# Streaming encoder layer with grouped experts: expert weights with neighbouring rows in one partition, and edits to mixing and routing

## What is computed

```
aff = sigmoid(h @ w_router);  sel = aff + router_bias            # 16 experts in 4 groups
group = argmax over groups of the sum of its two best sel
idx   = the 2 best experts inside that group;  w = aff[idx] / sum
y     = sum over e of gates[:, e] * ((silu(h @ w_gate[e]) * (h @ w_up[e])) @ w_down[e])
x     = x + g2 * y
```

## Time and profile before

| | us |
|---|---|
| median of 3 runs | 1313.42 |
| lowest and highest run | 1308.0, 1316.89 |
| the profiled execution | 1310.96 |
| its span (first to last instruction) | 1309.2 |
| mixing, first level to last copy of logits | 431.6 to 735.8 |
| routing, first operation to first gather | 737.5 to 771.0 |
| experts | 771.0 to the end |

### The profile page before, as it was taken

The page is one execution under the profiler, slowest core; times in us unless marked ns, Lnnn a source line. Parts: engine busy times, 40 slices in busy tenths (PEclk is TensorE's granted clock), DMA queues, the critical chain, the costliest instruction groups (busy, mean ns, idle before and its releaser), DMA issues. The chain is left out here.

```text
span 1309.2 us, 21577 instructions
## 1 busy us (share of the span) xinstructions
PE 1154.3 (88%) x6971; PEld 945.9 (72%) x6972; DVE 733.6 (56%) x1079; ACT 555.5 (42%) x930; POOL 346.4 (26%) x427
## 2 busy tenths in 40 slices
PE   4799999999786999999999249999999999899974
PEld 1688979988564777777777237888887887678863
DVE  0763500352355678777776574546195586656861
ACT  1664411333333355555553034324074364534750
POOL 1001100122322444334431020333332341333222
PEclk9799999999757999999999659999999999989987
DMA  9727673512183533332221583775779889897874
GB/s 347 285 91 266 230 279 109 175 48 73 55 231 99 144 109 109 110 110 86 78 88 54 184 314 121 239 236 176 205 241 366 255 262 354 285 336 242 263 284 96
DMA packets 119943, 249.88 MB, mean 191 GB/s; under 512 B 18225, under 2 KB 47665, under 8 KB 116802
## 3 DMA queue, kind: packets, MB, share of 16 engines
q1 hardware_dynamic: 107778, 204.92, 45.1%
q0 software_dynamic: 12096, 44.05, 12.8%
HBM read 205.02 MB, written 43.93 MB: 190 GB/s over the span
## 5 line engine op out<-in xcount | busy, mean ns | idle before, releaser
L2183 PE MATMUL psum<-e_w_h,e_x_h 128*128 128x512 f32 x432 | 173.9, 402 | 19.6 <-DVE w_gu L2296 12.8
L2185 PE MATMUL psum<-e_w_h,e_x_l 128*128 128x512 f32 x432 | 170.9, 395 | 0.0
L2184 PE MATMUL psum<-w_gu,e_x_h 128*128 x432 | 170.6, 395 | 0.0
L2130 POOL DMA_INDIRECT out<-e_work,e_to x26 | 81.0, 3117 | 298.2 <-DVE e_work L2284 298.2
L2296 DVE TENSOR_TENSOR w_gu<-w_gu,e_w_h 128x1024 f32 x128 | 146.9, 1218 | 11.5 <-ACT e_w_h L2239 11.5
L2239 ACT ACTIVATE e_w_h<-w_gu 128x1024 fp32r x128 | 123.3, 1048 | 46.2 <-issue 35.9
L2183 PEld LDWEIGHTS psum<-e_w_h,e_x_h 128*128 128x128 f32 x432 | 82.8, 192 | 37.8 <-DVE w_gu L2296 13.3
L503 PE MATMUL psum<-p_w_h,p_h_h 128*128 128x512 f32 (+1 forms) x288 | 105.8, 367 | 3.8 <-DVE p_h_l L659 3.8
L505 PE MATMUL psum<-p_w_h,p_h_l 128*128 128x512 f32 (+1 forms) x288 | 105.0, 364 | 0.0
L504 PE MATMUL psum<-p_w_l,p_h_h 128*128 128x512 f32 (+1 forms) x288 | 104.9, 364 | 0.0
L2185 PEld LDWEIGHTS psum<-e_w_h,e_x_l 128*128 128x128 f32 x432 | 82.5, 191 | 17.8
(11 more groups left out here) (389 smaller groups left out, 2484.8 us busy)
## 6 DMA issues: line engine op xcount, KB each, us to landing
w_gu<-in_w_e_gate SPq DMA_DIRECT2D x32, 1024.0 KB, 11.9
w_gu<-in_w_e_up SPq DMA_DIRECT2D x32, 1024.0 KB, 14.0
w_dn<-in_w_e_down SPq DMA_DIRECT2D x16, 2048.0 KB, 15.0
shared<-in_w_ada SPq DMA_DIRECT2D x24, 1024.0 KB, 6.5
p_w_raw<-in_w_in SPq DMA_DIRECT2D x5, 2048.0 KB, 9.3
tok_d<-p_tok SPq DMA_DIRECT2D x27, 256.0 KB, 2.0
feat_d<-p_work SPq DMA_DIRECT2D x12, 576.0 KB, 3.4
p_work<-in_x SPq DMA_DIRECT2D x9, 512.0 KB, 3.7
```

The costliest lines, as they stand in the source:

```text
L2183: pe.matmul(psum[:, j, :], x_h[:, k, :], wh, start=(k == 0), stop=False)
L2184: pe.matmul(psum[:, j, :], x_h[:, k, :], wl, start=False, stop=False)
L2185: last = pe.matmul(psum[:, j, :], x_l[:, k, :], wh, start=False, stop=(k == KC - 1))
```

## The change

The expert loads put rows 8p to 8p+7 of gate and up (a half: 8p to 8p+3 or 8p+4 to 8p+7), and rows 4p to 4p+3 of down, into partition p. To match, `turn_x` turns the columns 8r+k of the gathered rows, and `turn_u` the columns 4r+k of u. In mixing the diagonal goes to bank OB (columns 256 to 263), level 0 no longer waits for `pair_clear`, the diagonal waits for `rec_kept`, and `turn4(OB, k_d)` stands ahead of level 6. In routing the bias is loaded in mixing, the tile counts are added by one scan over a matmul result ordered by expert, the list matmuls are F32R with the gate as a high and a low part (product and rest on GpSimd, copy on ScalarE), the row number carries the "not empty" mark (it is one higher), and `at_place` is made last.

```
@@ load_expert
-        ks, rows = slice(half * KC // 2, (half + 1) * KC // 2), slice(half * D // 2, (half + 1) * D // 2)
+        ks = slice(half * KC // 2, (half + 1) * KC // 2)
         for j, w in enumerate((d["w_gate"], d["w_up"])):
-            sp.dma_start(b["w_gu"][:, par, j, ks, :], w[one(e), rows, :].rearrange("a (k p) n -> p (a k) n", p=P)).then_inc(b["gu_loaded"][par][half], 16)
+            sp.dma_start(b["w_gu"][:, par, j, ks, :], w[one(e), :, :].rearrange("a (p k) n -> p (a k) n", p=P)[:, ks, :]).then_inc(b["gu_loaded"][par][half], 16)
...
-    sp.dma_start(b["w_dn"][:, par, :, :], d["w_down"][one(e), :, :].rearrange("a (k p) n -> p (a k) n", p=P)).then_inc(b["dn_loaded"][par], 16)
+    sp.dma_start(b["w_dn"][:, par, :, :], d["w_down"][one(e), :, :].rearrange("a (p k) n -> p (a k) n", p=P)).then_inc(b["dn_loaded"][par], 16)
@@ experts, turn_x and turn_u
-                    last = pe.transpose(psum[:, 2 + k // 4, (k % 4) * P:(k % 4 + 1) * P], x_g[:, par, k * P:(k + 1) * P], ident[:, :])
+                    last = pe.transpose(psum[:, 2 + k // 4, (k % 4) * P:(k % 4 + 1) * P], x_g[:, par, :].rearrange("p (r k) -> p k r", k=KC)[:, k, :], ident[:, :])
...
-                    last = pe.transpose(psum[:, 4, k * P:(k + 1) * P], u[:, k * P:(k + 1) * P], ident[:, :])
+                    last = pe.transpose(psum[:, 4, k * P:(k + 1) * P], u.rearrange("p (r k) -> p k r", k=KD)[:, k, :], ident[:, :])
@@ mixing
+            sp.dma_start(b["bias"][:, :], router_bias.partition_broadcast(P)).then_inc(b["bias_loaded"], 16)
...
-                if i == 0:
-                    pe.wait_ge(s["pair_clear"], t + 1)
-                else:
+                if i == 0 and t:
+                    pe.wait_ge(s["state_ready"], t + 1)
+                if n:
                     pe.wait_ge(s["pair_ready"], n)
...
+                    if t:
+                        pe.wait_ge(s["rec_kept"], t)
-                last = pe.matmul(psum[:, M0, 2 * c:2 * c + 2], prod[:, c * P:(c + 1) * P], head_cols[:, :], start=True, stop=True)
+                last = pe.matmul(psum[:, OB, DIAG + 2 * c:DIAG + 2 * c + 2], prod[:, c * P:(c + 1) * P], head_cols[:, :], start=True, stop=True)
...
-                level(t, 6)
                 pe.wait_ge(s["kexp_ready"], t + 1)
                 if t:
                     pe.wait_ge(s["logit_ready"], t)
                 turn4(OB, k_d, s["kd_turned"])
+                level(t, 6)
@@ route, GpSimd and ScalarE
+            pool.wait_ge(s["in_list_ready"], 1)
+            pool.tensor_tensor(gate[:, :, :], in_list[:, :, :], bc(w_k[:, :, :].rearrange("p k t -> p (k t)"), 2, SLOTS),
+                               ALU.mult).then_inc(s["gate_ready"], 1)
+            pool.wait_ge(s["gate_high"], 1)
+            pool.tensor_tensor(entry[:, :, 2, :], gate[:, :, :], entry[:, :, 1, :].bitcast(F32), ALU.subtract).then_inc(s["gate_low"], 1)
...
+            act.wait_ge(s["gate_ready"], 1)
+            nc.scalar.activation(entry[:, :, 1, :], gate[:, :, :], ACT.Copy).then_inc(s["gate_high"], 1)
@@ route, TensorE
-            pe.matmul(psum[:, 1, 0:NT * NE], ones[:, :], flat, start=True, stop=True).then_inc(s["counted"], 1)
+            pe.matmul(psum[:, 1, 0:NT * NE], ones[:, :], both[:, :, :].rearrange("p t e -> p e t"), start=True, stop=True).then_inc(s["counted"], 1)
+            pe.wait_ge(s["gate_low"], 1)
@@ route, VectorE
-            link(dve.tensor_copy(tile_sum[:, :, :].rearrange("p t e -> p (t e)"), psum[:, 1, 0:NT * NE]))
-            for t in range(1, NT):
-                link(dve.tensor_tensor(before[:, t, :], before[:, t - 1, :], tile_sum[:, t - 1, :], ALU.add))
-            link(dve.tensor_tensor(count[:, :], before[:, NT - 1, :], tile_sum[:, NT - 1, :], ALU.add))
+            link(dve.tensor_tensor_scan(through[:, :, :].rearrange("p e t -> p (e t)"),
+                                        keep[:, :, :].rearrange("p e t -> p (e t)"), psum[:, 1, 0:NT * NE], 0.0, ALU.mult, ALU.add))
...
-            dve.tensor_tensor(at_place[:, :, :], ...)
-            link(dve.tensor_tensor(in_list[:, :, :], ...))
-            dve.tensor_copy(entry[:, :, 2, :], in_list[:, :, :])
+            dve.tensor_tensor(in_list[:, :, :], ...).then_inc(s["in_list_ready"], 1)
+            dve.wait_ge(s["in_list_ready"], 1)
...
-            dve.tensor_tensor(entry[:, :, 1, :], in_list[:, :, :], bc(flat(w_k[:, :, :]), 2, SLOTS), ALU.mult).then_inc(s["entries_ready"], 1)
+            dve.tensor_tensor(at_place[:, :, :], ...).then_inc(s["entries_ready"], 1)
...
-            dve.tensor_copy(b["list_gate"][:, :], psum[:, 2, SLOTS:2 * SLOTS])
+            link(dve.tensor_copy(b["list_gate"][:, :], psum[:, 2, SLOTS:2 * SLOTS]))
+            link(dve.tensor_tensor(b["list_gate"][:, :], b["list_gate"][:, :], psum[:, 2, 2 * SLOTS:3 * SLOTS], ALU.add))
```

More of the change, by code:

```diff
@@ L59 @@
 LISTS = 2 * NT + NE - 1
[L60 removed]
+SLOTS = LISTS + 3
 ENDS, LAST, SPLIT, NTH, INFO_W = SLOTS, SLOTS + NE, SLOTS + NE + 1, 2 * SLOTS + NE + 1, 3 * SLOTS + NE + 1
@@ L173, in stream_layer @@
             sampling(nc, b, d, sinks, state_in, s_sample)
-            mixing(nc, b, d, x, sinks, s_prompt)
+            mixing(nc, b, d, x, sinks, s_prompt, router_bias)
         b.update(
@@ L1117, in _, with mixing @@
             dve.tensor_tensor(o_n[:, :], o_n[:, :], gate, ALU.mult).then_inc(s["ob_ready"], 1)
-def mixing(nc, b, d, x, sinks, s_prompt):
+def mixing(nc, b, d, x, sinks, s_prompt, router_bias):
     psum, ident, logit = b["psum"], b["ident"], b["logit"]
@@ L1126, in mixing @@
     GAPS = 3
+    DIAG = 256
     NU = NT
@@ L1804, in _, with route @@
             keep_logits(u)
-def route(nc, b, d, router_bias):
+def route(nc, b, d):
     psum, ident = b["psum"], b["ident"]
@@ L1818, in route @@
         NG4 = NT * NG
-        bias = sb("bias", [P, NE])
+        bias = b["bias"]
         aff, sel, tmp = (sb(n, [P, NT, NE]) for n in ("aff", "sel", "tmp"))
@@ L1828, in route @@
         ones = sb("ones", [P, P])
-        tile_sum, before = sb("tile_sum", [P, NT, NE]), sb("before", [P, NT, NE])
-        count, n_list, end, first, ones_e = (sb(n, [P, NE]) for n in ("count", "n_list", "end", "first", "ones_e"))
+        keep, through = sb("keep", [P, NE, NT]), sb("through", [P, NE, NT])
+        n_list, end, first, ones_e = (sb(n, [P, NE]) for n in ("n_list", "end", "first", "ones_e"))
         steps = sb("steps", [P, NT])
@@ L1838, in route @@
         row_no = sb("row_no", [P, NT])
-        at_place = sb("at_place", [P, 2 * NT, P])
+        at_place = sb("at_place", [P, 2 * NT, P], F32R)
         in_list = sb("in_list", [P, 2 * NT, SLOTS])
-        entry = sb("entry", [P, 2 * NT, 3, SLOTS])
+        entry = sb("entry", [P, 2 * NT, 3, SLOTS], F32R)
+        gate = sb("gate", [P, 2 * NT, SLOTS])
         place_no, empty = sb("place_no", [P, P]), sb("empty", [P, SLOTS])
@@ L1849, in route @@
         kind = sb("kind", [P, SLOTS], I32)
-        names = "bias_loaded pool_made chain nlogit_ready e_ready counted both_ready entries_ready lists_made".split()
+        names = "pool_made in_list_ready gate_ready gate_high gate_low chain nlogit_ready e_ready counted both_ready entries_ready lists_made".split()
         s = {n: sem(n) for n in names}
@@ L1952, in _ @@
             link(dve.tensor_tensor(first[:, :], end[:, :], n_list[:, :], ALU.subtract))
-            link(dve.tensor_tensor(place[:, :, :].rearrange("p t e -> p (t e)"), psum[:, 0, 0:NT * NE],
-                                   before[:, :, :].rearrange("p t e -> p (t e)"), ALU.add))
+            link(dve.tensor_tensor(place[:, :, :], psum[:, 0, 0:NT * NE].rearrange("p (t e) -> p t e", e=NE),
+                                   through[:, :, :].rearrange("p e t -> p t e"), ALU.add))
             link(dve.scalar_tensor_tensor(out=place[:, :, :], in0=bc(first[:, :], 1, NT), scalar=float(P), in1=place[:, :, :],
@@ L1965, in _ @@
             flat = lambda ap: ap.rearrange("p k t -> p (k t)")
-            dve.tensor_tensor(at_place[:, :, :], bc(place_no[:, :], 1, 2 * NT), bc(flat(place_f[:, :, :]), 2, P), ALU.is_equal)
-            link(dve.tensor_tensor(in_list[:, :, :], bc(list_no[:, :], 1, 2 * NT), bc(flat(list_f[:, :, :]), 2, SLOTS), ALU.is_equal))
-            dve.tensor_copy(entry[:, :, 2, :], in_list[:, :, :])
+            dve.tensor_tensor(in_list[:, :, :], bc(list_no[:, :], 1, 2 * NT), bc(flat(list_f[:, :, :]), 2, SLOTS),
+                              ALU.is_equal).then_inc(s["in_list_ready"], 1)
+            dve.wait_ge(s["in_list_ready"], 1)
             for k in range(2):
```

36 lines of the change are left out of this document (20 added, 16 removed).

## The result

The changed kernel takes 1304.14 us (median of 20 runs, 1298.15 to 1310.15) where the kernel before takes 1310.97 (20 runs beside it). The ratio is 0.9947, with a 95% interval of 0.9936 to 0.9959: half a per cent faster, 7 us, which is within 1%. The forecast was 1290, 21 us faster. The profiled execution has a span of 1303.9 us against 1309.2.

A forecast was written before the change was run, and what follows sets the result against it. TensorE, busy 88% of the span, was taken to bound the kernel, so its waits cost time directly. 1311.0 us less 16 (stalls), 5 (routing) and 0.5 (mixing) gave 1289.5, called 1290; range 1281 to 1320, forecast's own 1281 to 1300.

The forecast's parts named there:

- Stalls: Expert stage: TensorE's four waits behind late weight loads, 27 us in all; longer packets were to save 16 us.
- small stall: Expert stage, two places losing 2.7 and 3.1 us behind a late w_dn load; 2.5 us each to be saved.
- 2.5 us earlier: w_dn's load took 11.08 us, 5.9 over the bare transfer; longer packets were to win back 2.5 of these.
- I cost that at nothing: Expert stage: weights' longer turns make POOL's gathers slower, but about a step of cover hides it; 0 us.
- rival D: Expert stage: gathers starve behind 16 KB packets and turn_x waits for x; 1306 us or more, chance 0.05.
- Column step: turn_x and turn_u: transposes reading columns 32 and 16 bytes apart instead of 4 cost 0, at most 46 us.
- Rivals A and B: Transposes doubling in time: all stepped ones (A, 1324 us, chance 0.14) or only the 32 byte step (B, 1314, 0.20).
- Routing: Routing stage: shorter counts, entry path and list matmuls sum to 6.0 us; 5.0 taken, as the first gather meets loads.
- The entry path: Routing, from the start of in_list to TensorE, gate product on POOL: 5.0 us against 5.4, saving 0.4.
- Mixing: Mixing stage: level 0's saved wait returns at level 1, k_d's turn nets 0.1 us a tile; 0.5 saved in all.
- Rival C: Expert loads keep 2 KB and 4 KB descriptors, or larger ones don't win turns; 1305.5 us, chance 0.13.

The follow-up runs named there:

- vec_gate: Changed kernel without its mixing edits, with routing's gate product and low part made by VectorE instead of GpSimd; 0.9923 of the kernel before.

## Why the prediction was wrong, point by point

**Stalls, predicted 16 saved, measured 11.0: the largest step that failed.** The mechanism stood: packet for packet, shares of a third and two thirds where both queues have work, as the row of 1138 to 1141 shows before and after. Over the whole of the large stall's loads, 1120 to 1138, POOL's queue is often empty and the shift is smaller: SP's queue moved 3.99 MB before and 4.65 after, POOL's 1.88 and 1.67. (The Trainium skill, "DMA: Bandwidth & Descriptors", section on queues, rings and completion order, has 9 to 17 descriptors to a turn; the equal counts at three run lengths, 220 to 215, 109 to 109 and 163 to 165, say one.) What failed is the size of the saving and where I put it. "In each small stall that is nearly all that was lost", from w_dn "2.5 us earlier": in the first small stall w_dn was issued at 973.21 and taken by ScalarE at 984.58 before, at 974.49 and 985.86 after.

```profile
974.49 0.33 SPq L193 DMA_DIRECT2D w_dn<-in_w_e_down  x1
...
985.86 3.90 ACT L2262 ACTIVATE e_w_dh<-w_dn  x4 [7.75 <-DMA w_dn<-in_w_e_down]
```

That is 11.4 us both times. I had read the 5.9 us over the bare load as lost turns. In those 11.4 us SP's queue moved 2.95 MB before and 3.15 after, and POOL's only 1.0 either way: there was little for longer packets to win back. SP's bytes were already more than w_dn's 2.1, so parts of w_gu moved while some parts of w_dn were still out. The small stalls went from 5.8 us to 3.5, the large ones from 21.2 to 12.5 (expected: 0.8 and 10.2). In the large one the 2.5 us came nearly whole: w_dn, issued at 1120.69 and taken at 1132.62 before, was issued at 1121.21 and taken at 1130.88, 2.3 us sooner. And w_gu was taken at 1138.32 after 2.14 us idle:

```profile
1130.88 3.90 ACT L2262 ACTIVATE e_w_dh<-w_dn  x4 [6.06 <-DMA w_dn<-in_w_e_down]
...
1138.32 3.90 ACT L2252 ACTIVATE e_w_h<-w_gu 128x1024 fp32r x4 [2.14 <-DMA w_gu<-in_w_e_up]
```

against 5.12 idle in the earlier trace rows. From 1138 to 1156 the two queues together moved some 413 to 423 GB/s, where it was 388 to 404: with the engines that full, no share of turns wins much more. And the forecast had no term for the clock. Of the 11.0 us some 2.3 are half clock that the first large stall no longer has (5.0 us in the stalls before, 2.7 after), so the longer packets themselves brought nearer 8.7.

**Gathers, "I cost that at nothing": the second step that failed, 3.4 us.** The cover of "about a step" was counted from the gather's step, not from its issue. POOL issues it only behind the preceding gates' gather, at 829.60 for a `turn_x` due at 841.8, a microsecond ahead of w_dn's load; 8.4 us of landing fit in those 12, 12.5 don't. This is rival D as a mechanism, given 0.05. I had argued against it with a cover that I should have read from POOL's rows. It did not eat the gain of the stalls, only a third of it; removing it by an early gather didn't pay.

**Column step, predicted 0, measured 1.5 us.** Rivals A and B fall. Weight loads of the transposes, from 780 to 1290 us (us, mean ns), first before, then after:

```profile
L2168 PEld LDWEIGHTS psum<-ident,e_work 128*128 128x128 f32 x216 | 25.2, 141 | 3.4
L2207 PEld LDWEIGHTS psum<-ident,e_work 128*128 128x128 f32 x108 | 13.0, 139 | 9.8 <-DVE e_work L2326 6.9
```

```profile
L2181 PEld LDWEIGHTS psum<-ident,e_work 128*128 128x128 f32 x216 | 28.1, 192 | 3.6 <-DMA e_work<-h_d,e_from 1.6
L2220 PEld LDWEIGHTS psum<-ident,e_work 128*128 128x128 f32 x108 | 17.0, 204 | 2.9 <-DVE e_work L2339 1.1
```

A load reads longer by some 50 to 65 ns, for the 16 byte step (L2220) as for the 32 byte step, but eight transposes take 0.89 instead of 0.87: most of the longer load lies beside other work. The Trainium skill ("SBUF — State Buffer", the section on the DMA port swizzle) would have the 16 byte step free and only the 32 byte one pay; here both paid alike, and little.

**Routing, predicted 5 of 6.0, measured 3.6 to list_row.** The scan saved 1.7, as forecast, and the bias wait 0.5. The list matmuls took 4.09 for 3.5. The entry path failed: "5.0 us ... against 5.4" became 6.8, because operations of both engines took longer there than alone: VectorE's own, as vec_gate shows, while for GpSimd's 3.37 us no run takes VectorE away. The row of a GpSimd operation in mixing could show neither. And of the 3.6, 0.35 was lost at the first gather and 1.3 in the first two steps. That last loss is TensorE's clock. The stretches of these two steps, before and after (the last three columns are granted clock, DMA share, GB/s):

```profile
775.60:792.70 17.10, 14.73 (x56) 11.91 (x57) 11.72 (x11) 9.27 (x10) 4.63 (x5) 0.76 0.35 117
792.70:807.20 14.50, 12.70 (x61) 10.32 (x60) 2.51 (x3) 2.22 (x3) 1.34 (x3) 1.00 0.11 36
```

```profile
773.30:790.10 16.80, 14.40 (x56) 11.75 (x57) 11.71 (x11) 9.27 (x10) 4.70 (x5) 0.78 0.38 121
790.10:806.30 16.20, 14.49 (x62) 11.73 (x61) 2.51 (x3) 2.22 (x3) 1.34 (x3) 0.89 0.11 32
```

In both kernels TensorE then waits 1.2 us for x; after the change the clock fell to 1.2 GHz behind that wait, before it didn't. Among the runs there are both kinds, with no edit at that place (a second step of 14.5 us in eight kernels, of 16.1 to 16.2 in six). So these 1.3 us can't be put down to the change.

**Mixing, predicted 0.5 saved, measured 1 lost.** Each step came, and the sign hung on 0.1 us. Level 6's fill saved 0.40 (for 0.44), but the diagonal stands 0.49 later behind it (for 0.35), and level 1 waits 0.71 longer (for 0.66) against 0.66 saved at level 0: 0.14 us a tile. VectorE's chain runs from the diagonal to level 1, 12.3 us in both kernels, so only the diagonal's time counts.

**The sum.** Predicted 16 + 5 + 0.5; measured 11.0 less 3.4 less 1.5 in the steps, routing through the second step 2.0, mixing -1.0, tail -1.6. Of these the clock is about +2.3, -1.3 and -1.6: it nearly cancels in the total, but it lies in three of the terms, and the forecast had it in none. Rival C's number, 1305.5, lies nearest to the result, for the wrong reason. The chance for "within 1%", 0.35, is the case that came; the range, 1281 to 1320, held it.

## What to carry to other kernels

When two DMA queues are busy at once, longer descriptors take bytes from the other queue: find what that other queue carries, when it is issued and when it is due, before costing its delay at nothing. Count a load's lost turns from the bytes that both queues moved in its own window, not from its duration over the bare transfer. Read the granted clock of each stretch before ascribing a difference of 2 us to an edit: one fall costs about that much, and one profile has it where the next has not. And where an edit moves one instruction and adds a wait for another, try the move alone.

## What the hardware showed unexpectedly

- **A gap ahead of `down` when `turn_x` is late.** TensorE then stands 0.3 to 0.8 us in a gap that no semaphore explains: 3 to 7 times in each of the seven kernels with 16 KB packets and POOL's old order, never in the four kernels that have the column step but no late gather. Between the two in TensorE's program stand two register loads from memory; whether these are the gap no run shows.
- **VectorE beside GpSimd.** VectorE's 324 column F32R products took 1.98 us for two beside GpSimd's product, and 0.89 when GpSimd was idle (vec_gate). GpSimd's 648 column difference took 3.37 us where its product of the same size took 1.58; both ran beside VectorE, so what slowed the difference is open.
- **Stalls grow when gathers come early**, by 7 us in two runs (22.8 and 22.6 against 16.0 and 15.5). Some 4.4 and 2.8 us of it is clock (the estimate from busy time at 0.50); which transfer is pushed back for the rest stays open.
- **The clock falls in some stalls and not in others.** At 0.50 for 10.2 us in the first large stall before, at 1.00 in the same stall after; in the tail at 1.00 before and at 0.50 for 3.3 us after, though TensorE waited for VectorE just ahead of it both times, 2.1 us before and 2.0 after.
- **SyncE's issues are shorter with long packets.** The last two ahead of the first large stall (L190) took 5.63 and 5.60 us before and 0.33 and 0.40 after. The DMA engines were busy throughout from 1126 to 1138 in the kernel before, so the long issues went with a full queue; whether they cost anything by themselves no run here shows.
